# The scores of block 2 as four single-pass products over 128 rows instead of two full-precision products over 64

## The reference, cut to what matters

```python
qa = rope(qa.reshape(B, Lp, SWA_Q_HEADS, HEAD_DIM), pos)     # 16 heads of 64, 4 heads of keys
ka = rope(ka.reshape(B, Lp, SWA_KV_HEADS, HEAD_DIM), pos)
qb = rope(qb.reshape(B, Lp, DIFF_HEADS, 2, HEAD_DIM), pos)   # 8 pairs of heads of 64
kb = rope(kb.reshape(B, Lp, DIFF_HEADS, 2, HEAD_DIM), pos)
...
s_band = jnp.einsum('bqhgd,bkhd->bhgqk', qi, kb) * scale     # branch 1, with mask and sink
s = jnp.einsum('bqhcd,bkhcd->bhcqk', qi, k) * scale          # branch 2, two softmaxes, subtracted
```

## Time and profile before

| | |
|---|---|
| median of three runs | 876.96 us |
| the profiled execution | 877.45 us, its span 875.6 us |
| TensorE busy | 868.0 us, 99% of the span |
| VectorE busy | 623.7 us, 71% |
| ScalarE busy | 459.2 us, 52% |
| granted TensorE clock | 0.998 |

### The profile page before, as it was taken

How to read it: one execution, slowest core, us unless ns; L and a number is a source line. 1 busy time by engine, 2 the same in 40 slices (tenths; PEclk the granted TensorE clock), 3 DMA queues, 4 the chain that set the end, 5 groups by cost and what they waited for, 6 DMA issues and landing times.

```text
span 875.6 us, 13035 instructions
## 1 busy us (share of the span) xinstructions
PE 868.0 (99%) x4820; PEld 731.3 (84%) x4820; DVE 623.7 (71%) x987; ACT 459.2 (52%) x735; POOL 46.2 (5%) x83
## 2 busy tenths in 40 slices
PE   9999999999999999999999999999999999999997
PEld 6887788888888888889998777777888888888886
DVE  6867777765876666668855888787766876666665
ACT  6546534334644444454556777677643654444443
POOL 1000010000200000002000000132300100000000
PEclk9999999999999999999999999999999999999999
DMA  9955344553565555353683335323274365555541
GB/s 328 412 207 187 129 160 144 192 192 144 190 242 190 189 195 188 142 190 104 207 300 106 123 123 170 145 100 142 97 265 175 119 228 189 183 192 192 186 143 48
DMA packets 26830, 156.75 MB, mean 179 GB/s; under 512 B 3600, under 2 KB 5136, under 8 KB 9376
## 3 DMA queue, kind: packets, MB, share of 16 engines
q1 hardware_dynamic: 24048, 148.71, 47.6%
q10 hardware_dynamic: 2736, 7.42, 2.4%
HBM read 151.45 MB, written 1.05 MB: 174 GB/s over the span
## 4 chain that ended last, share of the span: by engine, by line
PE 99%; DMA 0%; DVE 0%; DVEq 0%; SPq 0%; ACTq 0%; ACT 0%; issue 0%
PE ps L495 19%; PE ps L497 18%; PE ps L496 18%; PE ps L661 8%; PE ps L646 8%; PE ps L665 4%; PE ps L642 4%; PE ps L674 4%; PE ps L1639 2%; PE ps L676 2%; PE ps L530 1%; PE ps L1574 1%; PE ps L1598 1%; PE ps L1593 1%; PE ps L1588 1%; PE ps L1283 1%
## 5 line engine op out<-in xcount | busy, mean ns | idle before, releaser
L1742 DVE TENSOR_TENSOR wlo<-raw,whi 128x2048 fp32r<-128x2048 f32 x134 | 306.7, 2290 | 151.7 <-ACT whi L783 151.4
L783 ACT ACTIVATE whi<-raw 128x2048 fp32r<-128x2048 f32 x134 | 256.4, 1914 | 182.8 <-PE ps L497 110.8
L495 PE MATMUL ps<-whi,xT 128*128 128x512 f32 x192 | 76.8, 400 | 0.0
L497 PE MATMUL ps<-whi,xT 128*128 128x512 f32 x192 | 75.0, 391 | 0.0
L496 PE MATMUL ps<-wlo,xT 128*128 128x512 f32 x192 | 74.8, 390 | 0.0
L495 PE MATMUL ps<-whi,fT_h 128*128 128x512 f32 x128 | 50.2, 392 | 0.0
L496 PE MATMUL ps<-wlo,fT_h 128*128 128x512 f32 x128 | 49.8, 389 | 0.0
L497 PE MATMUL ps<-whi,fT_l 128*128 128x512 f32 x128 | 49.8, 389 | 0.0
L495 PE MATMUL ps<-x_all,whi 128*128 128x272 f32 x160 | 46.6, 291 | 0.0
L496 PE MATMUL ps<-x_all,whi 128*128 128x272 f32 x160 | 46.2, 289 | 0.0
L497 PE MATMUL ps<-x_all,wlo 128*128 128x272 f32 x160 | 46.2, 289 | 0.0
(11 more groups left out here) (347 smaller groups left out, 1834.5 us busy)
## 6 DMA issues: line engine op xcount, KB each, us to landing
raw<-weights SPq DMA_DIRECT2D x134, 1024.0 KB, 4.8
kswap<-kraw SPq DMA_DIRECT2D x52, 68.0 KB, 2.0
cst<-consts SPq DMA_DIRECT2D x1, 1371.0 KB, 13.0
raw<-weights SPq DMA_DIRECT2D x4, 256.0 KB, 5.5
raw<-weights SPq DMA_DIRECT2D x2, 512.0 KB, 7.2
gate_a<-gain_rows ACTq DMA_DIRECT2D x2, 512.0 KB, 7.7
gate_r<-gain_rows ACTq DMA_DIRECT2D x2, 512.0 KB, 6.7
gate_s<-gain_rows ACTq DMA_DIRECT2D x2, 512.0 KB, 6.6
```

What stands on the lines that cost most here:

```text
L495: pe.matmul(o, lh, rh, start=first, stop=False)
L497: return pe.matmul(o, ll, rh, start=False, stop=last)
L783: act.activation(whi[s][:], raw[s][:], ACT.Copy).then_inc(split_hi, 1)
L1742: dve.tensor_tensor(wlo[s][:], raw[s][:], whi[s][:], ALU.subtract).then_inc(split_lo, 1)
```

## The change

- The weights of block 2's queries and keys are reordered on the host, so that the two heads of a pair stand on alternate rows and the two halves of the rotation on rows 0 to 63 and 64 to 127. The swap is then two transfers of twice the size instead of four.
- The rotated sum goes back into `kswap` instead of a buffer of its own (signal `rot_ok`).
- ScalarE copies the sum, rounded, as a high part: once for keys (`keys_high`, into `knat`), twice for queries (`queries_high`, into both heads' buffers). VectorE subtracts it from the sum for a low part (`keys_rest`, `queries_rest`; signal `kt_ok`).
- SyncE's queue writes both parts of the keys to DRAM (`key_parts`, 5 times 0.56 MB) and reads them back, each row onto two neighbouring partitions, into two buffers `kB` of 0.56 MB (10 reads, each as two transfers). The low parts of queries go with two transfers of 0.13 MB onto the rows between the high parts.
- A unit's scores are then, for each of its two heads, one fp32r product over 128 rows with the keys' high part and one with their low part, added up in PSUM: four products where there were two.
- The units take both halves of the tokens one after the other, and the query and value blobs come in another order. Gate and up-projection blobs alternate by branch, and the loads of gate biases move from steps 13 and 40 to steps 38 and 54.

```diff
-QUERIES = (6, 7, 12, 13, 14, 15, 16, 17)
+QUERIES = (6, 7, 9, 10, 12, 13, 15, 17)
+QUERY_PLACE = (0, 1, 4, 2, 3, 5, 6, 7)
+VALUES = (5, 8, 11, 14, 16)
 SWAPPED = (0, 1, 2, 3, 4) + QUERIES
 
 
-VALUES_AT = {12: 0, 18: 1, 20: 2, 22: 3, 24: 4}
+VALUES_AT = {12: 0, 18: 1, 24: 2, 30: 3, 34: 4}
...
-    return 7 + i if i else 5
+    return VALUES[i]
...
-    return U % S_UNITS // 8 * 4 + U % 4, U % 8 // 4
-
-
-def query_made(U):
+    return U % S_UNITS // 2, U % 2
+
+
+def query_of(U):
 
     cc, _ = unit_place(U)
-    return 6 + U // S_UNITS * 4 + cc // 2
+    return U // S_UNITS * 4 + cc // 2
+
+
+def key_slot(U):
+
+    cc, _ = unit_place(U)
+    return cc // 4 if U < S_UNITS else cc % 2
+
+
+def keys_loaded(U):
+
+    cc, _ = unit_place(U)
+    return 32 if U < S_UNITS else 32 + 32 * (cc // 2 + 1)
...
-        kbT = new("kbT", [P, F_HEADS, KEYS])
-        ksT = new("ksT", [P, S_KV // 2, KEYS])
+        keys_at = top[0]
+        knat = [new("knat0", [P, 2, 2, KEYS], F32R), new("knat1", [P, 2, 2, KEYS], F32R)]
+        top[0] = keys_at
+        kB = [new("kB0", [P, 4, KEYS]), new("kB1", [P, 4, KEYS])]
+        rrow2 = at("rrow2", [P, TOK], F32, top[0])
+        ql = [new("ql0", [P, 2, TOK], F32R)]
...
+        qd = [None, at("qd1", [P, KC, TOK], F32R, region)]
...
-        qsT = new("qsT", [P, KC, TOK])
+        qs = [new("qs0", [P, KC, TOK], F32R), at("qs1", [P, KC, TOK], F32R, dead + 16)]
         gain_rows = at("gain_rows2", [P, 2, D], F32, top[0])
-        qbT = new("qbT", [P, KC, TOK])
+        qd[0] = new("qd0", [P, KC, TOK], F32R)
...
+        ql.append(new("ql1", [P, 2, TOK], F32R))
+        kd = nc.dram_tensor("key_parts", (5, P, 2, 2, KEYS), F32, kind="Internal").ap()
...
-                for g in range(4):
-                    o, s = g * 32, (g ^ 1) * 32
-                    sp.dma_start(kswap[b][o:o + 32], kraw[b][s:s + 32]).then_inc(ks_in[b], 16)
-
-            plain = N1 + 24
+                if swaps_before(m2):
+                    sp.wait_ge(kt_ok, max(SWAPPED.index(m) for m in SWAPPED if m < m2 and m % 2 == b) + 1)
+                sp.dma_start(kswap[b][0:DH], kraw[b][DH:P]).then_inc(ks_in[b], 16)
+                sp.dma_start(kswap[b][DH:P], kraw[b][0:DH]).then_inc(ks_in[b], 16)
+
+            def store_keys(i):
+
+                sp.wait_ge(kt_ok, i + 1)
+                parts = knat[i % 2][:].bitcast(F32)
+                if i:
+                    sp.dma_start(kd[i], parts).then_inc(kd_out[i % 2], 16)
+                else:
+                    sp.dma_start(kd[0, 0::2], parts[0::2]).then_inc(kd_out[0], 16)
+                    sp.dma_start(kd[0, 1::2, :, :, N_META:KEYS], parts[1::2, :, :, 0:TOK]).then_inc(kd_out[0], 16)
+                    sp.dma_start(kd[0, 1::2, :, :, 0:N_META], parts[1::2, :, :, TOK:KEYS]).then_inc(kd_out[0], 16)
+
+            def load_pair(r, i, cc):
+
+                for u in range(2):
+                    v = kd[i, u::2, cc].rearrange("d v k -> d (v k)").unsqueeze(1).to_broadcast([DH, 2, 2 * KEYS])
+                    o = kB[r][:, 2 * u:2 * u + 2, :].rearrange("p v k -> p (v k)")
+                    sp.dma_start(o, v).then_inc(kb_in[r], 16)
+
+            def load_shared_keys(r):
+
+                if r == 0:
+                    sp.wait_ge(kd_out[0], 16 * 5)
+                    sp.wait_ge(kd_out[1], 16 * 2)
+                load_pair(r, 0, r)
+
+            def load_keys(cc):
+
+                sp.wait_ge(u_sc, 2 * cc + 14 if cc else 8)
+                load_pair(cc % 2, 1 + cc // 2, cc % 2)
+
+            def store_queries(m2):
+
+                i = QUERIES.index(m2)
+                sp.wait_ge(kt_ok, 5 + i + 1)
+                j = QUERY_PLACE[i]
+                both = slice(2 * (j % 4), 2 * (j % 4) + 2)
+                for u, dst in enumerate(qs if j < 4 else qd):
+                    sp.dma_start(dst[1 - u::2, both, :].bitcast(F32),
+                                 ql[i % 2][u::2].bitcast(F32)).then_inc(q_in[j], 16)
+
+            plain = N1 + 30
             for n in range(N1, plain):
                 load(n, w[n], n - 2)
-                if n - N1 - 4 in SWAPPED:
-                    swap_halves(n - N1 - 4)
+                m = n - N1
+                if 6 <= m < 11:
+                    store_keys(m - 6)
+                if m in (12, 13):
+                    load_shared_keys(m - 12)
+                if m == 19:
+                    load_keys(0)
+                if 22 <= m < 29:
+                    load_keys(m - 21)
+                if m - 7 in QUERIES:
+                    store_queries(m - 7)
+                if m - 4 in SWAPPED:
...
-                    act.wait_ge(kt_ok, i - 1)
+                    act.wait_ge(rot_ok, i - 1)
...
+            def keys_high(i):
+
+                act.wait_ge(rot_ok, i + 1)
+                if i >= 2:
+
+                    act.wait_ge(kd_out[i % 2], 16 * (i // 2) + (0 if i % 2 else 32))
+                act.activation(knat[i % 2][:, :, 0], kswap[i % 2][:], ACT.Copy).then_inc(rot_hi, 1)
+
+            def queries_high(m2):
+
+                i = QUERIES.index(m2)
+                act.wait_ge(rot_ok, 5 + i + 1)
+                j = QUERY_PLACE[i]
+                for dst in qs if j < 4 else qd:
+                    m = act.activation(dst[:, 2 * (j % 4):2 * (j % 4) + 2, :], kswap[m2 % 2][:, :, 0:TOK], ACT.Copy)
+                m.then_inc(rot_hi, 1)
...
+                if q in (4, 6, 8, 10, 12):
+                    keys_high(q // 2 - 2)
+                if q % 2 == 1 and (q - 5) // 2 in QUERIES:
+                    queries_high((q - 5) // 2)
...
-                if q == 13:
+                if q == 38:
+                    act.wait_ge(u_sc, S_UNITS)
                     bias_rows(2, gate_s)
-                if q == 40:
+                if q == 54:
+                    act.wait_ge(u_sc, UNITS)
                     bias_rows(3, gate_d)
-                if q in (43, 47, 51, 55):
-                    g = (q - 43) // 4
-                    act.wait_ge(taken_d, taken_by(16 + 18 + g))
+                if q in (43, 47, 59, 63):
+                    g = (43, 47, 59, 63).index(q)
+                    act.wait_ge(taken_d, taken_by(16 + 18 + g + g // 2 * 2))
...
-                    pe.wait_ge(kt_ok, query_made(U))
+                    if t == 0:
+                        pe.wait_ge(q_in[query_of(U)], 32)
+                        pe.wait_ge(kb_in[key_slot(U)], keys_loaded(U))
                     if U:
                         pe.wait_ge(u_max, U)
                     if U > 5:
                         pe.wait_ge(d_lo, U - 5)
-                    qT = qsT if U < S_UNITS else qbT
+                    qT, kT = qs if U < S_UNITS else qd, kB[key_slot(U)]
                     for u in range(2):
-                        half = slice(u * DH, (u + 1) * DH)
-                        kT = ksT[half, cc // 4, :] if U < S_UNITS else kbT[half, cc, :]
-                        m = pe.matmul(ps[:, 4 + u, 0:KEYS], qT[half, cc, t * P:(t + 1) * P], kT, start=True, stop=True)
+                        for v in range(2):
+                            m = pe.matmul(ps[:, 4 + u, 0:KEYS], qT[u][:, cc, t * P:(t + 1) * P],
+                                          kT[:, 2 * u + v, 0:KEYS].bitcast(F32R), start=v == 0, stop=v == 1)
...
-                            if m2 == 26:
+                            if m2 == 22:
-                        xh, xl = (x2_h, x2_l) if m2 < 26 else (sT_h, sT_l) if m2 < 30 else (dT_h, dT_l)
+                        xh, xl = (sT_h, sT_l) if 22 <= m2 < 26 else (dT_h, dT_l) if m2 >= 30 else (x2_h, x2_l)
...
-                dst = (qsT if j < 4 else qbT)[:, 2 * (j % 4):2 * (j % 4) + 2, :]
-                dve.tensor_tensor(dst, raw_q, swap_q, ALU.add).then_inc(kt_ok, 1)
+                dve.tensor_tensor(swap_q, raw_q, swap_q, ALU.add).then_inc(rot_ok, 1)
+
+            def queries_rest(m2):
+
+                i = QUERIES.index(m2)
+                dve.wait_ge(rot_hi, 5 + i + 1)
+                if i >= 2:
+                    dve.wait_ge(q_in[QUERY_PLACE[i - 2]], 32)
+                j = QUERY_PLACE[i]
+                dve.tensor_tensor(ql[i % 2][:], kswap[m2 % 2][:, :, 0:TOK],
+                                  (qs if j < 4 else qd)[0][:, 2 * (j % 4):2 * (j % 4) + 2, :],
+                                  ALU.subtract).then_inc(kt_ok, 1)
+
+            def keys_rest(i):
+
+                dve.wait_ge(rot_hi, i + 1)
+                dve.tensor_tensor(knat[i % 2][:, :, 1], kswap[i % 2][:], knat[i % 2][:, :, 0],
+                                  ALU.subtract).then_inc(kt_ok, 1)
 
             def turned_keys(i):
 
                 b = i % 2
-                dve.wait_ge(ks_in[b], 64 * (i // 2 + 1))
+                dve.wait_ge(ks_in[b], 32 * (i // 2 + 1))
                 cs, sn = (turn[:, v, :].unsqueeze(1).to_broadcast([P, 2, KEYS]) for v in range(2))
                 dve.tensor_tensor(kraw[b][:], kraw[b][:], cs, ALU.mult)
                 link(dve, "dve", dve.tensor_tensor(kswap[b][:], kswap[b][:], sn, ALU.mult))
-                if i == 0:
```

(73 more changed lines are left out.)

6 lines of the change are left out of this document (3 added, 3 removed).

## The result

The changed kernel takes 890.43 us, the median of four runs (888.61 to 894.37); the kernel before took 877.04 us beside it (four runs). The ratio is 1.016, with a 95% interval of 1.0148 to 1.0173. It is slower, by 13.4 us where 4.5 were forecast, and lies above the range. The profiled execution took 890.27 us, 12.8 more than the one of before.

What follows compares the result with a forecast made beforehand. TensorE, busy 99%, was taken as the bound. From the profiled 877.45 us, - 9.2 (saving) + 12 (front waits) + 1.7 (keys' steps) gave 882.0, or 881.5 us as a median; range 878.5 to 885, 8 in 10 873.5 to 887.

Steps and rivals of the forecast that it cites:

- What bounds it, and the direction: Whole kernel: TensorE, busy 99%, is the bound; cheaper scores are outweighed by waits from list order, so slower, chance 0.72.
- The front waits: Unit steps: TensorE waits for VectorE's front at five steps, 10.8 us, plus 1.2 us for lateness afterwards; 12 us.
- Step 39's: Front wait at step 39, a step without value copies ahead of the high copies: 1.5 us.
- Blob 5: Keys' steps: TensorE waits 1.7 us near 427 us for VectorE's late split of blob 5; bounds 0.5 and 3.5 us.
- Blobs 6 to 8: Keys' steps: these blobs come out at least half a microsecond early, as blob 5's lateness gives them room.
- the transfers: Added DMA traffic, chiefly keys written to DRAM and read back: price 0, upper bound 5 us.
- The bounds of this stretch: Keys' steps: wait between 0.5 and 3.5 us, pushed up by a swap landing late behind the 0.56 MB key store.
- My rival on transfers: Reads of keys through DRAM wait behind weights: up to 5 us more, 886.5 us, chance 0.08; against it, 9 us of lead.
- The "about 8 MB" added: Transfers: 26 of 52 swap issues go and about 8 MB are added.
- The saving: Scores on TensorE: 0.36 us less per unit in branch 2, 0.21 in branch 1, 16 units each; 9.2 us together.
- The clock: Rival: TensorE's clock falls to 1.2 GHz after each of five front waits, 14.5 us more, 896 us; chance 0.02.

Runs made afterwards that it cites:

- the books with the waits undone: Shifts of blobs' ends against before: changed kernel with query copies behind the fronts, key stores in GpSimd's list, keys 4's swap ahead of blob 8's load; 872.94 us.

## Why the prediction came out low

- **What bounds it, and the direction: right.** TensorE was the bound, the scores got cheaper, and waits that the order of the lists makes ate more than that.
- **The front waits (forecast 12 us): right in mechanism.** The five are 10.6 us for 10.8, each at its step. Step 39's was the furthest off, 2.2 us for 1.5. Three smaller waits, ahead of values' transposes near 479 and 514 and of a turn near 571.6, make 1.7 more by the starts, where I had 1.2. With the low clock after the first wait, 1.6 us, the stretch holds 13.9 us. Moving the copies alone gave 13.7 back.
- **Blob 5 (1.7): right,** 1.70, with VectorE's split as releaser.
- **Blobs 6 to 8: the step that failed.** I wrote that they "come out at least half a microsecond early", and priced the transfers at 0. I had followed VectorE and ScalarE, but not what blob 5's lateness does in SyncE's list: the load of blob 8 goes out 2.5 us later and stands, with 0.54 MB of store, in front of a swap that is due in 4 us. Price: 4.2 us, of which 2.5 is the wait and 1.7 the low clock. That the load decides, far more than the store, is shown by the swap put ahead of one or of both: ahead of the store alone it was still late, ahead of both it landed after 2.3 us. The bounds of this stretch did name a late swap, but behind the store and as a delay of blob 5. My rival on transfers looked at the reads of keys, 9 us of lead; none of those ever made TensorE wait. The swap has no such lead. The "about 8 MB" added were also too few: SyncE's queue moved 159.17 MB for 148.71, since the queries' low parts (2.1 MB) were left out. No run shows a cost of that.
- **The saving (9.2): mis-sized.** By the books with the waits undone it is 6.35, or 7.0 with the 0.6 us wait left in that kernel. Branch 2 gives 0.32 us a unit by the shift of the blobs' ends (0.64 for two) for the forecast 0.36; branch 1 some 0.15 for 0.21. The local count of starts gives more, 0.35 and 0.16, 8.2 in all, near the 8.1 of the run with the scores' products alone changed. In branch 1 the term failed on the four products, which take 0.61 us to the next blob's first where the sum had 0.56. Of the 1.2 us between 8.2 and 7.0 half lies in branch 2, where a step takes 4.70 us before, 4.34 with the scores' products alone changed and 4.38 here. Its twelve products of half a blob take 2.76 us, for 2.73 with the scores alone changed. Where the rest lies stays open.
- **The clock (chance 0.02): underrated.** It fell after two of the seven waits of over a microsecond, for 3.3 us together. Over the profiled runs of all kernels with waits, all five waits of 2.7 us or more (to 5.0) came with a low stretch, nine of 22 between 1.7 and 2.6 us did, and none of the twelve between 1.2 and 1.5. The Trainium skill (TensorE: Matmul & The Clock Gate, "HAM oscillation — how this bites in real kernels") speaks of gaps that throttle the engine again, by the example of waits of 3 to 5 us. These runs agree that a gap can do it, and show that a shorter one can be enough and need not be. What decides between them is not settled.

In sum: 4.5 forecast; 4.2 for blob 7, 2.2 for the saving, 1.9 for the fronts and their clock and 0.2 at blob 4, where the split was late too, bring it to 13.

## What to carry to other kernels

A new operation that waits for another engine belongs behind whatever in its list TensorE waits for soonest; the same six copies and subtractions cost 13 us ahead of the front and next to nothing behind it. When an edit delays one engine, follow the delay into the list of the queue that loads: which large transfer now goes out late, and which small, urgent one stands behind it. When a transfer is moved, ask also who waits for what it leaves behind, since the store that was passed held its own buffer 4 us too long.

## What the runs showed of the hardware

- A transfer of 136 KB within the chip took 2.2 us from issue to landing at best in the keys' steps, 3.5 to 4.3 with 0.54 MB beside it in another engine's list, 6.2 to 6.8 with a megabyte ahead of it in its own list and 0.54 MB beside it, and 7.0 to 7.3 with both ahead of it in its own.
- TensorE's starts fell from 0.21 to 0.43 us apart after waits of 2.40 us (twice in the profiled run), for 1.7 and 1.6 us of loss, and kept their pace after 2.1 to 2.2 us. In another kernel they fell after 1.80 us and not after 2.40. The share of the clock differs from run to run of one kernel (0.991 to 0.997 over the four of the change), and with it the time, 894.37 to 888.61.
